# A second square in the first down stage, with the rotary angles moved into the retention stage

## What is computed

```python
def swiglu(x, w_gate, w_up, w_down):
    return (jax.nn.silu(x @ w_gate) * (x @ w_up)) @ w_down     # widths: 1024 to 2816 to 1024

def rope(t, positions):
    half = t.shape[-1] // 2
    inv = ROPE_BASE ** (-jnp.arange(half, dtype=jnp.float32) / half)
    ang = positions.astype(jnp.float32)[..., None] * inv
    cos = jnp.cos(ang)[:, :, None, :]
    sin = jnp.sin(ang)[:, :, None, :]
    t1, t2 = t[..., :half], t[..., half:]
    return jnp.concatenate([t1 * cos - t2 * sin, t1 * sin + t2 * cos], axis=-1)

# in first_block, layer 0:
f = swiglu(rmsnorm(h, g[0]), ffn_w_gate[i, 0], ffn_w_up[i, 0], ffn_w_down[i, 0])
h = h + FFN_RES_WEIGHT * rmsnorm(f, g[1])
m = retention(rmsnorm(h, g[2]), positions, ret_w_in[j], ret_gn_gain[j], ret_w_out[j])
# retention: q, k, v, g = split(h @ w_in); rope on q and k of 4 heads of width 256;
# scores * decay, times v; normalised, gated by silu(g), @ w_out
```

## Time and profile before

| | |
|---|---|
| median of 3 runs | 1358.76 us (1358.66 to 1359.29) |
| the profiled execution | 1358.57 us |
| its span, first to last instruction | 1356.8 us |
| PE busy | 1352.3 us (100%) |
| VectorE busy | 1061.8 us (78%) |
| ScalarE busy | 754.3 us (56%) |
| GpSimd busy | 158.9 us (12%) |
| HBM read | 260.20 MB, 193 GB/s over the span |

### The profile page before, as it was taken

One profiled execution on the slowest core, in us unless ns is written; L12 is line 12 of the kernel. 1 busy time (PEld: TensorE's weight loads), 2 busy tenths in 40 slices (PEclk: granted clock), 3 DMA queues, 4 the chain that ended last, 5 costly groups with the idle time before them and its releaser, 6 DMA issues.

```text
span 1356.8 us, 19494 instructions
## 1 busy us (share of the span) xinstructions
PE 1352.3 (100%) x6923; PEld 1149.5 (85%) x6923; DVE 1061.8 (78%) x1232; ACT 754.3 (56%) x1025; POOL 158.9 (12%) x190
## 2 busy tenths in 40 slices
PE   9999999999999999999999999999999999999999
PEld 8888888888888888888888888888888888888887
DVE  6888877888668999777999754678999776577765
ACT  6454555444354447574446566654547665545674
POOL 1211010000012110121110011122110110002100
PEclk9999999999999999999999999999999999999999
DMA  8865647555647765648764654458665556545431
GB/s 262 261 200 186 217 139 247 195 174 182 201 134 260 236 211 168 208 150 288 235 204 172 219 186 142 157 163 270 219 202 198 196 171 202 181 165 183 159 125 63
DMA packets 188872, 262.20 MB, mean 193 GB/s; under 512 B 15579, under 2 KB 115971, under 8 KB 188803
## 3 DMA queue, kind: packets, MB, share of 16 engines
q1 hardware_dynamic: 184476, 246.50, 55.8%
q0 software_dynamic: 4032, 14.68, 3.2%
q10 hardware_dynamic: 295, 0.13, 0.0%
HBM read 260.20 MB, written 1.05 MB: 193 GB/s over the span
## 4 chain that ended last, share of the span: by engine, by line
PE 96%; DVE 2%; ACT 1%; POOL 0%; issue 0%; DVEq 0%; ACTq 0%; POOLq 0%
PE sums L937 13%; PE sums L641 13%; PE sums L643 13%; PE sums L642 13%; PE turn L937 11%; PE sums L944 7%; PE turn L944 6%; PE turn L641 2%; PE turn L643 2%; PE turn L642 2%; PE turn L795 1%; DVE w_lo L1964 1%; PE turn L897 1%; PE turn L896 1%; PE turn L895 1%; PE sums L897 1%
## 5 line engine op out<-in xcount | busy, mean ns | idle before, releaser
L1964 DVE TENSOR_TENSOR w_lo<-raw,w_hi 128x1024 fp32r<-128x1024 f32 x452 | 569.6, 1297 | 101.2 <-ACT w_hi L1445 99.6
L1445 ACT ACTIVATE w_hi<-raw 128x1024 fp32r<-128x1024 f32 x452 | 464.4, 1054 | 235.5 <-DMA raw<-in_ffn_w_up_dram 92.2
L937 PE MATMUL sums<-x_both,w_hi 128*128 128x512 f32 x768 | 183.6, 391 | 0.0
L937 PEld LDWEIGHTS sums<-x_both,w_hi 128*128 128x128 f32 x768 | 141.3, 188 | 27.5
L641 PE MATMUL sums<-w_hi,y_hi 128*128 128x512 f32 x398 | 156.9, 394 | 0.0
L641 PE MATMUL sums<-w_hi,x_both 128*128 128x512 f32 x392 | 155.4, 396 | 0.0
L643 PE MATMUL sums<-w_hi,y_lo 128*128 128x512 f32 x398 | 155.1, 390 | 0.0
L642 PE MATMUL sums<-w_lo,y_hi 128*128 128x512 f32 x398 | 155.0, 389 | 0.0
L643 PE MATMUL sums<-w_hi,x_both 128*128 128x512 f32 x392 | 152.9, 390 | 0.0
L937 PE MATMUL turn<-x_both,w_hi 128*128 128x512 f32 x640 | 152.7, 391 | 0.0
L642 PE MATMUL sums<-w_lo,x_both 128*128 128x512 f32 x392 | 152.6, 389 | 0.0
(11 more groups left out here) (304 smaller groups left out, 1864.4 us busy)
## 6 DMA issues: line engine op xcount, KB each, us to landing
raw<-in_ffn_w_gate_dram SPq DMA_DIRECT2D x175, 256.0 KB, 3.7
raw<-in_ffn_w_up_dram SPq DMA_DIRECT2D x175, 256.0 KB, 4.4
raw<-in_ffn_w_down_dram SPq DMA_DIRECT2D x162, 256.0 KB, 3.9
raw<-in_ret_w_in_dram SPq DMA_DIRECT2D x96, 256.0 KB, 3.9
raw<-in_conv_w_in_dram SPq DMA_DIRECT2D x64, 256.0 KB, 3.9
raw<-in_attn_w_in_dram SPq DMA_DIRECT2D x64, 256.0 KB, 3.9
raw<-in_sb_w_in_dram SPq DMA_DIRECT2D x48, 256.0 KB, 4.0
raw<-in_ret_w_out_dram SPq DMA_DIRECT2D x32, 256.0 KB, 3.8
```

What stands on the lines that cost most here:

```text
L937: pe.matmul(banks[:, fc, :], w_hi[:, (n0 + s - s0) % RING, c, fc * P:(fc + 1) * P], x_both[:, SC * s + c, :, :].rearrange("p h t -> p (h t ...
L1445: act.activation(w_hi[:, n % RING].rearrange("p c n -> p (c n)"), slot_source(n).rearrange("p c n -> p (c n)"), ACT.Copy).then_inc(hi_made, 1)
L1964: dve.tensor_tensor(w_lo[:, n % RING].rearrange("p c n -> p (c n)"), slot_source(n).rearrange("p c n -> p (c n)"), w_hi[:, n % RING].rearr ...
```

## The change

The first down stage gets two squares, as the others have: the square of row 8 keeps its weight sums in `work`, a new one of row 6 keeps them in the spare memory. The sum of y_hi and y_lo that a square other than row 8 needs is then made in stage 0 too, so the count waited for is f + 1. As weight sums now stand in `work` from column 1536 on, the frequencies, the positions and the late gains move to columns 1024 to 1535. `angles` leaves the first down stage for the retention stage, on VectorE ahead of the first head's `qk_sums`; `sines` stands on ScalarE ahead of the first head's gates.

```diff
@@ -68,8 +68,8 @@
 MW_Q, MW_K, MW_V, MW_Z, MW_QT, MW_KT = 0, 1024, 2048, 3072, 4096, 5120
 MW_HEAD, MW_DIST, MW_SQ = 6144, 7680, 8064
 TW = 1536
-AW_FREQ, AW_ANGLE, AW_K, AW_KH, AW_POS, AW_POSF = 1536, 1792, 2048, 2304, 2816, 3072
-GW = 2688
+AW_FREQ, AW_POS, GW = 1024, 1152, 1408
+AW_ANGLE, AW_K, AW_KH, AW_POSF = 1792, 2048, 2304, 3072
 WORK = 8704
 
 
@@ -111,7 +111,7 @@
 
 
 
-PAIRS = {0: [(8, "spare")], 1: [(8, "work"), (6, "spare")], 2: [(8, "work"), (6, "spare")], 3: [(8, "work"), (6, "spare")]}
+PAIRS = {0: [(8, "work"), (6, "spare")], 1: [(8, "work"), (6, "spare")], 2: [(8, "work"), (6, "spare")], 3: [(8, "work"), (6, "spare")]}
 
 
 
@@ -1522,8 +1522,6 @@
                     fn()
                 if ph.f is not None:
                     seven_copies(ph)
-                    if ph.f == 0:
-                        sines()
                 split_to(free)
                 if read:
                     read(0)
@@ -1678,6 +1676,8 @@
                     act.wait_ge(mx["r_turned"], 1)
                     act.activation(work[:, RW_R:RW_R + SEQ], turn[3][:, 0:SEQ], ACT.Copy).then_inc(mx["r_flat"], 1)
                 split_to(s0 + 16)
+                if hd == 0:
+                    sines()
                 if hd:
                     ret_y_hi(hd - 1)
                 ret_gates(hd, 0)
@@ -2041,8 +2041,6 @@
                     fn()
                 if ph.f is not None:
                     seven_sums(ph)
-                    if ph.f == 0:
-                        angles()
                 split_to(free)
                 first(0)
                 then(0)
@@ -2067,7 +2065,7 @@
                         rows = slice(SC * row, SC * row + 2 * SC)
                         dve.tensor_tensor(work[:, at:at + 1024].rearrange("p (c t) -> p c t", c=2 * SC), y_hi[:, rows, :].bitcast(F32),
                                           y_lo[:, rows, :].bitcast(F32), ALU.add).then_inc(y_added, 1)
-                        dve.wait_ge(y_added, f)
+                        dve.wait_ge(y_added, f + 1)
                     a1, a2 = (work[:, at + 512 * i:at + 512 * (i + 1)].rearrange("p (c t) -> p c t", c=SC) for i in range(2))
                     a11, a21, a12, a22 = a1[:, :, 0:P], a1[:, :, P:SEQ], a2[:, :, 0:P], a2[:, :, P:SEQ]
                     s1, s2, s3, s4 = (work[:, HW_S[pair] + 256 * m:HW_S[pair] + 256 * (m + 1)].rearrange("p (c t) -> p c t", c=SC)
@@ -2378,6 +2376,8 @@
                 if hd:
                     finish(hd - 1)
                 split_to(s0 + 14)
+                if hd == 0:
+                    angles()
                 qk_sums(hd)
                 if hd:
                     ret_y_lo(hd - 1)
```

## The result

The changed kernel takes 1362.05 us (median of 15 executions, 1360.89 to 1363.82) where the kernel before, run on the same chip, takes 1358.84 us (15 executions, 1358.26 to 1359.52). The ratio is 1.0023 [1.0017, 1.003]: 3.2 us slower. The profiled execution took 1361.97 us with a span of 1359.9 us, against 1358.57 and 1356.8 before.

The account below looks back on a forecast made before the run. TensorE, busy 1352.3 of 1356.8 us, bounds the kernel. The square's -1.36 us plus 4.2 us of waits gives +2.9 us (rounded up) on the 1358.76 us median, stated as 1361.6 us, range 1360.0 to 1363.3.

Parts of the forecast that it names:

- Part 1, the square: First down stage: the second square drops one of 43 products, six matmuls on PE, for -1.36 us.
- In `down0` they cost PE nothing: First down stage: the angles cost PE nothing there, so moving them out gives nothing back.
- Part 2, the slide: Retention stage, first head: angles ahead of `qk_sums(0)` make VectorE's later work start 7.6 us later, with no idle time absorbing it.
- The chain through ScalarE and GpSimd: Sines, table multiplication and gates of head 0: wait at `rope(0)` 0 to a few tenths, gates 0.5 us early, no table load.
- (a) The first wait: Slot s0+14, first head of retention: PE waits 2.8 us for VectorE's low split, 0.25 us of restart included.
- (d) The second wait: `ret_mix(0)`: the low part of `weights(0)` comes late, another 1.4 us, making 4.2 us in all (3.7 to 4.4).
- (e) The turn of the rows: PE's turn of head 0's rows: 8.1 us of room for 7.6, so no third wait, but nearly one.
- Only the first wait: Rival, chance 0.14: loads of s0+18 and s0+19 land quickly, `weights(0)` is in time, only 2.8 us stay: 1360.2 us.
- hidden: Rival, chance 0.09: VectorE reaches the angles early enough in the retention stage that both waits fall away: 1357.4 us.
- lack of room: Rival, chance 0.11: the start or `down0` lacks room for the square, one more wait of 1.2 us: about 1363.0 us.
- 43 products: Rival, chance 0.02: the square saves nothing, as if PE still ran 43 products in `down0`: 1363.0 us.
- The clock falls: Rival, chance 0.04: two waits drop PE to 1.2 GHz for one group of 24 matmuls (5.44 us): about 1367 us.

Follow-up runs that it names:

- the repeat: The changed kernel run and profiled once more, with nothing altered: 1361.71 us, ratio 1.0021.
- angles in the expand stage: Changed kernel, both squares kept, with the 19 angle steps two by two in the first expand stage and sines in `down0`: 1357.27 us, ratio 0.9989.
- shorter block: Changed kernel with six of the eight steps that subtract multiples of two pi left out of the angles: 1358.95 us, ratio 1.0001.
- one wait, filled: Kernel of weights ahead plus nine pairs of small constant matmuls on PE before slot s0+14: 1360.5 us, ratio 1.0012.
- square alone: Kernel before plus the second square in the first down stage, angles and sines left there: 1359.89 us, ratio 1.001.
- two splits ahead: Changed kernel with the low splits of slots s0+14 and s0+15 directly behind the angles, before the first head's sums: 1360.87 us, ratio 1.0011.
- weights ahead: Changed kernel with head 0's weights before the low splits of slots s0+18 and s0+19 on VectorE: 1361.56 us; once more, 1361.58 us.
- two waits, the first filled: Changed kernel plus nine pairs of small constant matmuls on PE before slot s0+14: 1363.26 us; once more, 1362.62 us.
- angles alone: Kernel before, one square kept, with only the angles and sines moved into the retention stage: 1362.71 us, ratio 1.0027.
- longer block: Changed kernel with four more steps that subtract zero added to the angles: 1363.41 us, ratio 1.0033.

## Why the prediction was right, and where it was off

The time was 1362.05 us against 1361.6 predicted, in the range of 1360.0 to 1363.3, with the measured +0.23% on the side of the line that had 0.53; its interval, +0.17 to +0.30%, reaches over that line. By its own steps:

- **Part 1, the square.** Predicted -1.36 us, measured -1.35 us, with PE busy throughout `down0` and no wait in the expand stage. The bound of 1.2 us for a lack of room in the start was not needed: 6.8 us more of VectorE work in the expand stage (99.86 us against 93.08 us in the same window of the kernel before) left it at 111.4 us.
- **"In `down0` they cost PE nothing."** True of the kernel before and false of the kernel that the change makes: with two squares they would cost 2.6 us there. It didn't enter the sum, but a reader who compares places for the angles needs it. The move is no free choice to be judged on its own; it is what the square asks for.
- **Part 2, the slide.** Predicted 7.6 us, measured 7.57 us. As far as the weights the stretches behind it kept their lengths within 0.2 us in the profile above. That is partly luck, because in the repeat the stretch that ends with loads took 8.20 us instead of 9.00. Behind the weights the sentence that the later idle times absorb nothing was wrong: the low part of the weights ends 6.41 us later than in the old trace (240.46 and 234.05 us), the rows of head 0 only 4.71 us later (251.62 and 246.91), so 1.7 us were absorbed.
- **The chain through ScalarE and GpSimd.** No wait at `rope(0)`, which starts 0.22 us after the table is ready, no table load, no wait for the gates' bank. GpSimd started 0.07 us behind the sines, where I had allowed 0.15 us without a row. Tight, and right in this profile; in the repeat PE comes 0.11 us late to that bank (224.18, due 224.07), and four more steps overdraw it by 1.1 us.
- **(a) The first wait.** Predicted 2.8 us, measured 2.51. The restart was mis-sized: I added 0.06 us and a weight load of 0.19 us, and PE was back 0.04 us after the split ended (228.06 + 1.23 to 229.33), and 0.06 us after the low weights (239.90 + 0.56 to 240.52). The weight load doesn't come on top; what there is instead is 0.11 us between the first two matmuls.
- **(d) The second wait.** Predicted 1.4 us, measured 1.54; the two together 4.2 and 4.05. But their sum is firmer than the split: the repeat of the same kernel has 2.99 and 0.73 us (restarts at 230.03, and at 240.42 where 239.69 was due), 3.72 in all. The start of the block differs between executions by up to 0.7 us, which the prediction took from one profile as if it were fixed. The range covered it by its 3.7 to 4.4 us.
- **(e) The turn of the rows.** No wait: the rows end at 250.93 + 0.69 = 251.62 and are wanted at 253.81, 2.2 us of room where I had counted on 0.5; the difference is the 1.7 us absorbed.
- **The rivals.** "Only the first wait", "hidden", "lack of room" and "43 products" are each refuted by a row above. **"The clock falls"** is where the prediction was wrong on the mechanism. I gave it 0.04 and 1367 us. In the executions here the mean clock was below 1.000 in 11 of 15 and 6 of 8 of the changed kernel, so it happens most of the time; but one fall slows some nine matmuls and costs 1.5 to 1.7 us, not the 5.4 us of a whole group of 24, and most of it disappears in the second wait. By the Trainium skill's page "TensorE: Matmul & The Clock Gate" (Part 1, on the two states), that idleness of the array halves its clock, I had put 1367 if 2.8 us count as idle and 1361.6 if not. The traces agree with the rule at 2.0 to 2.9 us of idle time, in a part of the executions, and the time still came out near the second number, because the step that turned the rule into us was wrong and the slack of the second wait hid the rest. The forecast was therefore a little luckier than its argument. "The granted clock stays full", as the sign of a right prediction, held in the profiled execution and not in most others.

For the profiled execution I had 1361.5 and it took 1361.97 us. The 0.5 us between them are 0.3 us outside the span, 0.22 us of restarts and 0.14 us of the later expand stage, less 0.15 us by which the waits were smaller and the 0.06 us that I had rounded up. The restarts come with every such wait. The start of the expand stage is variation: it lies between 19.50 and 20.14 us in the other profiles.

## What to carry to other kernels

When TensorE is busy for 99% of the time, a block of work on another engine is priced by the first due time behind it in that engine's queue, not by the engine's share: compute start of the block + its length + what follows, and compare it with when PE wants the result. The same 7.6 us cost 2.6 us in one place, 4.1 us in another and nothing when they were dealt out in pairs over a stage with slack; so cut chained side work into pieces before looking for one hole that holds it all. And where one wait hides another, removing the first may gain nothing: list the waits in order, with what sets each, before valuing one.

## What the runs showed of the hardware

- **A single idle time of 2.0 to 2.9 us of TensorE can halve its clock.** The mean clock of the executions, PE's waits from each profile (one execution each, and they vary), and how far the median time of the executions below 1.000 lies above that of the others:

| kernel | waits of PE in this stretch, us | executions below 1.000 | apart by, us |
|---|---|---|---|
| before; angles in the expand stage | none new | 0 of 85; 0 of 11 | |
| shorter block | 0.6 and 0.8 | 0 of 10 | |
| one wait, filled | 0.8 and 0.5 | 0 of 11 | |
| square alone | 2.4 | 3 of 11 | 1.87 |
| two splits ahead | 2.0 | 5 of 10 | 1.86 |
| weights ahead, both runs | 2.1; 2.7 | 12 of 20 | 1.77; 2.05 |
| two waits, the first filled, both runs | 0.8 and 1.4; 0.8 and 2.0 | 4 of 11 | 1.58; 2.79 |
| angles alone | 2.7 and 1.2 | 3 of 7 | 0.00 |
| after, both runs | 2.4 and 1.4; 2.8 and 0.6 | 17 of 23 | 0.39; 0.12 |
| longer block | 1.1 and 2.9 | 5 of 6 | 0.16 |

  Every trace that caught a fall has it at a wait of 2.0 to 2.9 us, and no execution fell in the kernels whose waits were 0.8 us or less. In the traces a fall costs 1.5 to 1.7 us (the 2.79 us is one execution, whose loads also landed late). In the kernel with one wait, matmuls of constants in the idle time prevented it.
- **Two-input work of VectorE beside GpSimd's:** a split took 2.34 us instead of 1.22 us beside a multiplication of 1.47 us, and another 2.68 us beside one of 1.30 us. The same multiplication cost sums that read PSUM nothing.
- **Sines and Silu without a table load:** on ScalarE the sines stand directly ahead of the gates, with no load between them in either order of work.
